# Distance tables and head biases built in the first up projection, and attention opened with the first half of the tokens

## The reference

```python
x = x + _rms_norm(mix, g[1])                                # mix: convolution, then attention
ff = _swiglu(_rms_norm(x, g[2]), ffn_in_w[layer], ffn_out_w[layer])
x = x + _rms_norm(ff, g[3])
...
bias = -slopes[:, None, None] * (delta * dilation).astype(jnp.float32)[None]
sc = jnp.where(valid[:, None, None], sc + bias, -jnp.inf)   # per branch and head
...
DILATED_GROUPS = ((128, 1), (512, 4), (2048, 16))           # window, dilation
```

## Time and profile before

| | |
|---|---|
| Median of three runs | 2272.85 us (2272.17 to 2273.74) |
| Profiled execution, own time | 2273.41 us |
| its span, first to last instruction | 2271.6 us |
| granted TensorE clock, mean | 0.997 |
| TensorE busy | 2216.3 us (98%) |
| VectorE busy | 1687.8 us (74%) |
| ScalarE busy | 962.3 us (42%) |
| GpSimd busy | 485.1 us (21%) |
| bytes read from memory / written | 202.40 MB / 48.76 MB |

### The profile page before, as it was taken

The page is one execution under the profiler, slowest core; times in us unless marked ns, Lnnn a source line. Parts: engine busy times, 40 slices in busy tenths (PEclk is TensorE's granted clock), DMA queues, the critical chain, the costliest instruction groups (busy, mean ns, idle before and its releaser), DMA issues. The chain is left out here.

```text
span 2271.6 us, 31865 instructions
## 1 busy us (share of the span) xinstructions
PE 2216.3 (98%) x10604; PEld 1848.8 (81%) x10604; DVE 1687.8 (74%) x2529; ACT 962.3 (42%) x1758; POOL 485.1 (21%) x416
## 2 busy tenths in 40 slices
PE   7999998999999999999999999999899999999997
PEld 6888887888888888877888888888788888888886
DVE  6988769777777667797767666676877777776768
ACT  4322345322222243564566566565532222223453
POOL 5000026333333100251110011002533333310113
PEclk9999999999999999999999999999999999999999
DMA  5122242333333477635333233234133333338764
GB/s 158 38 56 56 96 155 61 102 108 98 111 98 112 157 265 241 204 122 161 84 85 84 67 73 83 57 107 144 50 113 107 102 104 105 103 108 281 246 227 171
DMA packets 246010, 278.24 MB, mean 122 GB/s; under 512 B 18528, under 2 KB 157792, under 8 KB 243808
## 3 DMA queue, kind: packets, MB, share of 16 engines
q1 hardware_dynamic: 242656, 264.84, 38.0%
q10 hardware_dynamic: 3200, 11.54, 1.5%
HBM read 202.40 MB, written 48.76 MB: 111 GB/s over the span
## 5 line engine op out<-in xcount | busy, mean ns | idle before, releaser
L1249 PE MATMUL banks<-xb_mid,up_split 128*128 128x512 f32 x2064 | 477.4, 390 | 1.5 <-DVE up_split L2381 1.5
L1249 PEld LDWEIGHTS banks<-xb_mid,up_split 128*128 128x128 f32 x2064 | 388.2, 188 | 82.5 <-DVE up_split L2381 1.9
L1338 PE MATMUL banks<-down_split 128*128 128x512 f32 x1848 | 423.0, 390 | 4.7 <-DVE down_split L2749 3.3
L1338 PEld LDWEIGHTS banks<-down_split 128*128 128x128 f32 x1848 | 345.4, 188 | 80.9 <-DVE down_split L2749 8.1
L1249 PE MATMUL banks<-xb_low,up_split 128*128 128x512 f32 x1584 | 368.8, 391 | 5.6 <-DVE xb_low L2309 2.0
L1249 PEld LDWEIGHTS banks<-xb_low,up_split 128*128 128x128 f32 x1584 | 298.1, 188 | 69.0 <-DVE up_split L2381 4.8
L2749 DVE TENSOR_TENSOR down_split<-down_raw,down_split 128x1024 fp32r<-128x1024 f32 x154 | 198.2, 1287 | 107.3 <-ACT down_split L1955 106.9
L1955 ACT CAST down_split<-down_raw 128x1024 fp32r<-128x1024 f32 x154 | 161.8, 1051 | 204.2 <-PE banks L1338 169.5
L3391 POOL TENSOR_TENSOR sums<-raw_up 128x512 f32<-128x512 f32 x88 | 117.3, 1336 | 482.3 <-DMA raw_up<-in_ffn_in_w 255.1
L1383 PE MATMUL banks<-x_hi,w_second 128*128 128x512 f32 x672 | 176.3, 394 | 0.0
L3062 DVE CUSTOM_DVE_ANT_0 scores<-banks,bias 128x896 f32<-128x896 f32 (+7 forms) x128 | 96.7, 756 | 78.8 <-PE banks L1420 63.5
(11 more groups left out here) (227 smaller groups left out, 3607.8 us busy)
## 6 DMA issues: line engine op xcount, KB each, us to landing
raw_up<-in_ffn_in_w SPq DMA_DIRECT2D x88, 512.0 KB, 5.0
down_raw<-in_ffn_out_w SPq DMA_DIRECT2D x154, 256.0 KB, 3.4
down_raw<-hid_spill SPq DMA_DIRECT2D x154, 256.0 KB, 4.1
hid_spill<-hid_mix SPq DMA_DIRECT2D x110, 256.0 KB, 4.9
down_second<-in_ffn_out_w SPq DMA_DIRECT2D x66, 256.0 KB, 3.3
k_stack<-k_parts SPq DMA_DIRECT2D x32, 512.0 KB, 6.2
hid_spill<-hid SPq DMA_DIRECT2D x44, 256.0 KB, 2.0
raw_up<-in_conv_in_w SPq DMA_DIRECT2D x18, 512.0 KB, 5.2
```

Source lines behind the costliest of these rows:

```text
L1249: mm = pe.matmul(bank(b_out), up_part(ph, p, a)[:, q * P:(q + 1) * P], block(RIGHT_OF[p], b)[:, q, :], start=(i == 0), stop=(i == len(pass ...
L1338: mm = pe.matmul(bank(b_out), side[:, a, 0, i * P:(i + 1) * P], side[:, b, 1, :], start=(p in (M3, M5, M1, M2) and first and j == 0), stop ...
```

## The change

The tables move from the opening of attention into sets 3 to 13 of the first up projection, where `resid` is kept in memory for a while (`x_keep`) and its place in SBUF holds the tables. All 16 head biases are made there, as whole rows of 1024, in two buffers by turns, and stored to memory (`bias_spill`, 8 MB); the third of three in an odd set writes the buffer of the first. The residual is loaded back in sets 15 to 18. In attention a bias is loaded by SyncE into one of two buffers, one for each head of a pair, when the last maximum on it is done, and VectorE waits for that load at a change of head; `head_bias`, `last_bias` and the slopes go.

The opening's order becomes keys, values, queries of the first half and then of the second, with the tiles turned later; the low part of the weights is waited for only in the third pass. The scaling (GpSimd) and splits of the query weights and the first key split move into `norm2`; SyncE loads the first two biases and stacks the queries of the first half ahead of the keys. ScalarE runs one Exp on a dummy before the last query split of the opening.

```diff
+        dist_i = at(112, "dist_i", [SEQ], I32)
+        neg_log = at(116, "neg_log", [SEQ])
...
+        head_table = at(136, "head_table", [2, SEQ])
...
-        OPENING = ((0, 0), (1, 0), (0, 1), (2, 0), (1, 1), (2, 1))
-        TURNS = {22: HT, 36: HT + 1, 46: HT + 2, 48: HT + 3}
+        OPENING = ((0, 0), (1, 0), (2, 0), (0, 1), (1, 1), (2, 1))
+        TURNS = {28: HT, 40: HT + 1, 52: HT + 2, 62: HT + 3}
...
+        TABLE_SETS, TABLE_PARTS, TILES_BACK = range(3, 14), 6, {15: (0, 1), 16: (2, 3), 17: (4, 5), 18: (6, 7)}
+
+        def table_parts(n):
+
+            before = 4 * ((n - 3) // 2) + (3 if n % 2 == 0 else 0)
+            return before, {2: 0, 3: 1, 4: 2} if n % 2 and n < 13 else {2: 0, 3: 1} if n % 2 else {3: 0}
...
                 load_set(up, layer, 1)
+                if layer == 0:
+                    for t in range(TT):
+                        sp.wait_ge(*x_new_right.at("norm1", t + 1))
+                        sp.dma_start(x_keep[t], resid[:, t, :]).then_inc(kept, 16)
                 for n in range(FT - 1):
...
                         store_mixed(up, n - 1)
+                    if layer == 0 and n in TABLE_SETS:
+                        before, places = table_parts(n)
+                        for j in range(before, before + len(places)):
+                            if j >= TABLE_PARTS:
+                                head = j - TABLE_PARTS
+                                sp.wait_ge(*bias_made.at("up0", head + 1))
+                                sp.dma_start(bias_spill[head], head_table[:, head % 2, :]) \
+                                    .then_inc(bias_out[head % 2], 16)
+                    if layer == 0 and n in TILES_BACK:
...
+                            sp.dma_start(resid[:, t, :], x_keep[t]).then_inc(x_back, 16)
                     store_hidden(up, n)
...
+            def load_bias(r, e):
+
+                moving, fixed = r
+                if fixed:
+                    sp.wait_ge(*max_done.at("attn", moving * STEPS + (fixed * STEPS - (1 - e) * TT)))
...
+                sp.dma_start(att["bias"][:, e, :], rows[bass.ds(moving * (2 * P) + (2 * fixed + e) * P, P), :]) \
+                    .then_inc(bias_in[e], 16)
...
-            for pos in range(2, 5):
+            for pos in range(2, 4):
                 load_projection(pos, 0)
+            sp.wait_ge(*xt_turned.at("norm2", TT))
+            for e in range(2):
+                load_bias((0, 0), e)
+            queries_first(0)
+            load_projection(4, 0)
             stack_first()
...
                     stack_keys((g * 2, pp + 1), 0)
+                    load_bias((g * 2, pp + 1), 0)
                     load_projection(8 + 3 * pp, g)
...
                     stack_keys((g * 2, pp + 1), 1)
+                    load_bias((g * 2, pp + 1), 1)
...
+                if i == 2 * KT and h == 0:
+                    pe.wait_ge(*lo_ready.at("attn", part + 1))
                 if i == 0:
                     if h == 0:
-                        pe.wait_ge(*lo_ready.at("attn", part + 1))
+                        pe.wait_ge(*hi_ready.at("attn", part + 1))
...
             values_high((0, 0), 1, TURN)
+            act.activation(table_junk[:], neg_half[:], ACT.Exp)
             project((0, 0), 5, OPENING)
...
+            def table_part(j):
+
+                if j == 0:
+                    distances()
+                    window_counts(0)
+                elif j < 3:
+                    window_counts(j)
+                elif j == 3:
+                    masked_logs()
+                elif j < TABLE_PARTS:
+                    log_of(j - 2)
+                else:
+                    head = j - TABLE_PARTS
+                    if head >= 2:
+                        dve.wait_ge(bias_out[head % 2], 16 * (head // 2))
+                    dve.scalar_tensor_tensor(out=head_table[:, head % 2, :], in0=dist,
+                                             scalar=2.0 ** (-(head % 2 + 1) / 2 - head // 2), in1=logs,
+                                             op0=ALU.mult, op1=ALU.add).then_inc(bias_made.sem, 1)
...
                         mix(ph, {1: M5, 2: M1, 3: M7, 4: M2}[p], n // 2 - 1)
+                    if layer == 0 and n in TABLE_SETS:
+                        before, places = table_parts(n)
+                        if p in places:
+                            table_part(before + places[p])
...
                 if pre:
+                    project((0, 0), 0, OPENING)
+                    low_part(norm_ph, HT)
                     normed(norm_ph, TT - 2)
-                    low_part(norm_ph, HT)
+                    prepare(chunk0["attn"] + 2)
                     normed(norm_ph, TT - 1)
...
-                    other_head = s + 1 in (TT, STEPS)
-                    if other_head:
-
-                        dve.wait_ge(*max_done.at("attn", steps + (s + 1)))
-                        head_bias(moving, fixed + (s + 1) // STEPS, (s + 1) // TT % 2, 0)
+                    if s + 1 in (TT, STEPS):
+                        dve.wait_ge(bias_in[(s + 1) // TT % 2],
+                                    moving * 16 + 16 * (fixed + (s + 1) // STEPS + 1))
                     negated_scores(steps, s + 1)
...
-            distances()
-            window_counts(0)
-            window_counts(1)
             project((0, 0), 2, OPENING)
...
+                    if ph == "up0" and n == 2:
+                        pool.wait_ge(kept, 16 * TT)
...
+                        pool.iota(dist_i[:], pattern=[[-1, SEQ]], base=SEQ - P, channel_multiplier=1) \
+                            .then_inc(dist_ready.sem, 1)
                     weight_sums(ph, n)
```

More of the change, by code:

```diff
@@ L1989, in up_layer, with project @@
                 split_high(down, 2)
+            def project(r, pos, order=ORDER):
+                moving, fixed = r
+                part, h = order[pos]
+                b = PROJ + pos % 2
+                cols = slice(h * HALF, (h + 1) * HALF)
+                product("attn", h, moving * 3 + (3 * fixed + part + 1),
+                        moving * 3 + (3 * fixed + part + 1))
+                if part == 0:
+                    for e in range(2):
+                        if fixed and h == 0:
+                            act.wait_ge(k_stacked[e], moving * 32 + fixed * 32)
+                    act.copy(att["k_parts"][:, 0, cols], bank(b)) \
+                        .then_inc(k_hi_done.sem, 1)
+                elif part == 1:
+                    act.wait_ge(*v_turned.at("attn", moving * 2 + (2 * fixed + h)))
+                    act.copy(att["v_t"][:], bank(b)).then_inc(v_done.sem, 1)
+                else:
+                    for e in range(2):
+                        if fixed or h:
+                            act.wait_ge(q_stacked[e], moving * 64 + (2 * fixed + h) * 32)
+                    act.activation(att["q_parts"][:, 0], bank(b), ACT.Copy,
+                                   scale=-float(HD) ** -0.5).then_inc(q_hi_done.sem, 1)
             def down_layer(ph, norm_ph):
@@ L2075, in _ @@
             act.dma_start(x_spill.rearrange("t p d -> p t d"), resid[:]).then_inc(spilled, 16)
[L2077 to L2090, removed]
-                elif part == 1:
-                    act.wait_ge(*v_turned.at("attn", moving * 2 + (2 * fixed + h)))
-                    act.copy(att["v_t"][:], bank(b)).then_inc(v_done.sem, 1)
-                else:
-                    for e in range(2):
-                        if fixed or h:
-                            act.wait_ge(q_stacked[e], moving * 64 + (2 * fixed + h) * 32)
-                    act.activation(att["q_parts"][:, 0], bank(b), ACT.Copy,
-                                   scale=-float(HD) ** -0.5).then_inc(q_hi_done.sem, 1)
             def values_high(r, h, b=PROJ + 1):
@@ L3452, in scale_pair @@
                     scale_chunk(3 * (fixed + 1) + c, moving if isinstance(moving, int) else moving * 3)
[L3454 removed]
+            pool.wait_ge(*xl_ready.at("norm2", TT))
+            for c in (3, 4):
                 scale_chunk(c)
```

220 lines of the change are left out of this document (104 added, 116 removed).

## The result

| | before | after |
|---|---|---|
| runs of the comparison, median (lowest to highest), us | 2273.58 (2271.22 to 2274.63) | 2281.72 (2277.75 to 2286.2) |
| profiled execution, us | 2273.41 (span 2271.6) | 2281.51 (span 2279.7) |
| granted clock, mean | 0.997 | 0.996 |

The ratio after to before is 1.0039, 95% interval 1.003 to 1.0049. The change makes the kernel slower by 0.4%, some 8 to 9 us (the medians lie 8.1 apart), where 2274.4 was predicted and 2279.5 was the upper end. What was won in the opening of attention is less than what the first up projection and, against the forecast, the attention loop lose.

What follows compares the result with a forecast made beforehand. TensorE, busy 98% of the span, was taken as the bound, so only its waits count. Opening -4.2, attention -1.2 and up projection +7.0 sum to +1.6 on the profiled 2273.41; on the median 2274.4, range 2266.5 to 2279.5.

Steps and rivals of the forecast that it cites:

- +7.0: First up projection: tables and head biases make VectorE late and stall TensorE, 7.0 us lost; ends 0 and +9.5.
- a slack of 3.6 us: Up projection: VectorE may be 3.6 us late at the sum freeing the first product's bank before TensorE stalls.
- The first rival: Up projection: no stall, as the first head's store lands by 438 or parts fit into waits; 2267.4 us, chance 0.26.
- -4.2: Opening of attention: new product order and earlier keys, less late query weights, gain 4.2 us; ends -7.2 and 0.
- 4.2 us at full clock: Opening: work from first to third score product, 15 matmuls and two score products, claimed to take 4.2 us.
- the 1.3 us that should have been given back: Opening: ScalarE waits 2.6 us for late query weights at their split, idle time absorbs part, 1.3 us are lost.
- The lower bound, -7.2: Opening: best end of the term, with keys in time and no block at the query weights, 7.2 us gained.
- -1.2: Attention: head biases leave VectorE, saving two thirds of TensorE's 1.8 us last-pair wait, 1.2 us; ends 0 and -2.5.
- the weight load behind them: Attention: the load behind SyncE's two added bias loads for each pair, claimed to be due only a pair later.
- the third rival: Up projection: table work meets GpSimd's sums some eight times, 1.1 us each, 5 of 9 us reaching TensorE; 2279.4, chance 0.08.
- The copy of the residual in the up projection and its way back: Up projection: the 4 MB copy to memory and its reload in sets 15 to 18 were taken to cost nothing.

Runs made afterwards that it cites:

- the three kernels above: Changed kernel with 24 memsets starting VectorE's program (2280.26 us); with the last pair's weight load ahead of its bias (2280.32); with three head-table buffers, table work in odd sets (2271.79).
- the copy cut in two: Changed kernel with the residual's 4 MB copy on ScalarE's queue cut in two, finished tiles going out some 45 us earlier: 2278.17 us, ratio 1.0024.
- the combined kernel: Changed kernel with three head-table buffers, odd sets, second bias late, last pair's weight load ahead of its bias, residual's copy cut in two, 24 memsets: 2266.16 us, ratio 0.997.
- the kernel with three buffers: Changed kernel with a third buffer for the head tables, so an odd set's third head no longer waits for the first's store: 2275.61 us, ratio 1.0012.

## Why the prediction was wrong

**Up projection: right in its mechanism, 7.9 where +7.0 was worked out.** The mechanism is the one that the prediction named: the bank of product 0, a slack of 3.6 us, three waits of VectorE for a store, in sets 7, 9 and 11. By the set in which it was made, the loss is 1.68 behind set 4 (0.8 predicted), 0.02 behind set 5, 1.27 behind set 6 (0.45), 4.97 behind sets 7 to 12 (5.7). An even set costs 1.2 to 1.35 instead of 1.44, an odd one 0.33 to 0.40 instead of 0.45. The part mis-sized is what sets 3 and 5 leave behind, 1.7 us in all: VectorE's sum ended 3.1 us late in set 3, not 2.1, and set 5, which was to win back 1.0, won back nothing. Two collisions with GpSimd, told below, have just this size. The first rival (no stall) falls: the store of the first head is not there in time.

**Opening: right in its mechanism, -3.6 where -4.2 was worked out.** The projections gain 5.3 us (4.8 predicted). The keys land 0.85 us later than predicted (1054.69 - 8.24 = 1046.45 in the time of before, for 1045.6, in which half a MB at the residual's rate should be 1.6, not 1.7). From there to the third score product the prediction has 4.2 us at full clock: it took 5.7, with the half speed behind the wait. So the gain at the third score product was 3.2 for 5.5. Against that, the 1.3 us that should have been given back by late query weights were not: ScalarE waited 1.44 us for them, but TensorE did not stand for it, and by 1106 it had won another 0.4. Errors of 2.3 and -1.7 nearly cancel here, but both belong to this execution. In the three kernels above where the clock stayed up behind the same wait, the stretch took 4.5 to 4.9 us, ScalarE then waited 2.0 to 2.3 us for the query weights, and TensorE gave back 0.6 to 1.0; their openings gain 3.7 to 4.1 us by the same matmul. So both terms were right in kind, 4.2 some 0.5 too low and 1.3 some 0.5 too high. The lower bound, -7.2, is what the copy cut in two reaches, alone and in the combined kernel.

**Attention: wrong, the step that puts the time out of the range.** -1.2 was worked out, with ends 0 and -2.5; to the end of the kernel it is +3.4. With -1.2 there the time would be near 2277, inside the range. The wait for VectorE's output columns in the last pair, from which the gain was taken, shrank from 1.8 to 1.4 only, 0.4 us. The 4.2 us lost up to the last pair have two causes, neither in the list. One is the second pause behind the jump back (1.1 and 1.9 us). Nothing in the prediction costs what moving instructions does to the place of the loop in VectorE's program; a row that points there is VectorE's wait named "issue" at the jump, 2.19 us in the kernel before, which the prediction left out. The other is SyncE's order in the last pair (1.2 us): the prediction weighed the added loads against "the weight load behind them", which is due a pair later in the loop, and left out the last pair, which has its own order, and where VectorE splits that weight some 10 us behind its issue.

**Collisions: the third rival falls in its size, not in its mechanism.** It reckoned with eight meetings of table work and GpSimd's sums. There were two, in sets 3 and 5, and each cost VectorE 1.0 to 1.1 us, the price that it had. In set 3 (timelines of VectorE and of GpSimd):

```profile
439.56 1.22 DVE L2872 TENSOR_TENSOR counted<-counted 128x1024 f32<-128x1024 f32 x1
440.82 1.67 DVE L2443 TENSOR_TENSOR up_split<-raw_up,up_split 128x512 fp32r<-128x512 f32 x1
...
446.44 0.69 DVE L2964 TENSOR_TENSOR third_gate<-second_up,banks 128x512 f32<-128x512 f32 x1
```

```profile
439.65 2.29 POOL L3437 TENSOR_TENSOR sums<-raw_up 128x512 f32<-128x512 f32 x1 [6.53 <-DMA raw_up<-in_ffn_in_w]
...
489.93 1.30 POOL L3437 TENSOR_TENSOR sums<-raw_up 128x512 f32<-128x512 f32 x1 [4.47 <-DVE up_split L2443]
```

The table step began first and took its usual 1.22. GpSimd's sum, 0.09 us later, took 2.29 for 1.30, and the split behind the step, begun while the sum ran, took 1.67 for 0.69. In set 5 a split took 1.78 in the same way, behind a head table; all 16 head tables themselves took 1.21 to 1.23. In the kernel with three buffers the sum began first, and the table step paid:

```profile
439.00 2.28 DVE L2873 TENSOR_TENSOR counted<-counted 128x1024 f32<-128x1024 f32 x1
```

```profile
438.91 1.29 POOL L3438 TENSOR_TENSOR sums<-raw_up 128x512 f32<-128x512 f32 x1 [6.35 <-DMA raw_up<-in_ffn_in_w]
```

From 446.44 + 0.69 and the set's first matmul at 426.14 the sum ends 20.99 us into set 3, for 17.93 in the earlier trace rows: the 3.1 us late of above, 1.0 more than was worked out without the collision. No run took the collisions away by itself.

**The copy of the residual in the up projection and its way back: right.** No wait of TensorE or VectorE names them.

## What to carry to other kernels

Work moved under a busy engine is paid in the consumer's slack, so cost it set by set, and look for what keeps a late engine from catching up: here not the 32 us of added work but one buffer too few, worth 4.5 us, and two collisions with another engine that came before it. Where a load is added to a queue that a loop and a tail both use, check the tail's own order and whatever large copy shares the engines at that moment; a copy whose data is ready earlier should go earlier. And after any edit to an engine whose loop is on the critical path, look at its pauses without a cause behind the jump: a few instructions more or less ahead of the loop decided 2 to 3 us.

## What was unexpected

- A second pause of 1.5 to 2.8 us after a loop's jump, always 13 instructions behind it, made by 12 instructions that do nothing and taken away by 24.
- Half speed behind a stall comes in some executions and not in others. In three of the five profiled executions with a series of stalls, not in that of the changed kernel, some eight matmuls in set 9 took twice their time, 1.65 us, behind idle times of 1.82, 2.09 and 2.41 us; behind 1.8 us in set 5 of the kernel with three buffers none did. In the opening idle times of 2.36 (before), 2.40 and 2.69 us were followed by it, 2.47, 2.51 and 2.66 were not. What decides was not found.
- With the DMA engines full (1.05 busy behind the projections), two MB moved out of the stretch brought the keys 3.2 us sooner after their issue, and half a MB behind them instead of ahead the first score product 1.05 us.
